# One-hot products of the gate stage as three bf16 products in place of one in float32

## The reference

```
s1, s2 = q[:, :, 0] @ k1.T, q[:, :, 1] @ k2.T          # 8 heads, 128 keys each
v1, i1 = top_k(s1, 16);  v2, i2 = top_k(s2, 16)
top_s, pos = top_k(v1[..., :, None] + v2[..., None, :], 16)
idx = i1 * 128 + i2   (of the chosen pairs)
g = softmax(top_s)                                     # 8 x 16 = 128 experts a token
y = sum over the 128 experts e:  g_e * gelu(x . u[idx_e]) * v[idx_e]
```

## Time and profile before

| | |
|---|---|
| time, median of 3 runs | 1710.99 us (1710.89 to 1716.2) |
| the profiled execution | 1710.73 us, span of its instructions 1708.9 us |
| TensorE busy, products / loads | 1635.4 us (96%) / 1420.3 us (83%) |
| VectorE, ScalarE, GpSimd busy | 1256.0 (73%), 644.1 (38%), 836.6 us (49%) |
| mean granted clock of TensorE | 0.988 |
| share of the last chain | PE 59% (L1620 30%, L845 22%, L833 5%, L1498 3%) |
| gate stage | about 540 to 1004 us; first loop from 600, second from 795 us |

### The profile page before, as it was taken

The page is one execution under the profiler, slowest core; times in us unless marked ns, Lnnn a source line. Parts: engine busy times, 40 slices in busy tenths (PEclk is TensorE's granted clock), DMA queues, the critical chain, the costliest instruction groups (busy, mean ns, idle before and its releaser), DMA issues.

```text
span 1708.9 us, 23340 instructions
## 1 busy us (share of the span) xinstructions
PE 1635.4 (96%) x8522; PEld 1420.3 (83%) x8522; DVE 1256.0 (73%) x2452; ACT 644.1 (38%) x1056; POOL 836.6 (49%) x542
## 2 busy tenths in 40 slices
PE   7999889699998999999999889999999999999996
PEld 5876644499998999999999888888888888888885
DVE  6667842368998988855886357778777778888876
ACT  3568740333424433432333233333333333333331
POOL 4734520194454378877877524445555563222201
PEclk9999999899999999999999999999999999999999
DMA  8436300433345578898789989998999989999972
GB/s 274 147 104 191 99 0 0 139 101 105 118 130 168 156 203 228 228 320 244 214 227 254 356 298 321 323 323 321 320 326 326 318 298 346 350 356 351 360 250 101
DMA packets 242897, 397.16 MB, mean 232 GB/s; under 512 B 33704, under 2 KB 173408, under 8 KB 242784
## 3 DMA queue, kind: packets, MB, share of 16 engines
q1 hardware_dynamic: 182816, 259.17, 44.6%
q0 software_dynamic: 55296, 134.31, 26.1%
q10 hardware_dynamic: 4672, 2.19, 0.5%
HBM read 349.40 MB, written 46.20 MB: 231 GB/s over the span
## 4 chain that ended last, share of the span: by engine, by line
PE 59%; DVE 4%; DMA 2%; POOL 1%; issue 1%; ACT 1%; SPq 0%; POOLq 0%; DVEq 0%; ACTq 0%
PE bank L1620 30%; PE bank L845 22%; PE bank L833 5%; PE bank L1498 3%; DMA u_raw<-in_peer_u 2%; POOL gate_matrix L213 1%; DVE sel_late L954 1%; DVE ut_lo L903 1%; POOL gathered L1005 0%; DVE hit_late L952 0%; DVE hit_late L945 0%; DMA gathered<-in_peer_u,expert_rows 0%; DVE gather_product L1017 0%; ACT L975 0%; DVE first L1422 0%
## 5 line engine op out<-in xcount | busy, mean ns | idle before, releaser
L845 PE MATMUL bank<-xhi,ut_hi 128*128 128x384 f32 x1024 | 354.4, 346 | 0.3 <-ACT gel L871 0.3
L845 PE MATMUL bank<-xhi,ut_lo 128*128 128x384 f32 x1024 | 344.2, 336 | 0.0
L845 PE MATMUL bank<-xlo,ut_hi 128*128 128x384 f32 x1024 | 344.0, 336 | 0.0
L1005 POOL DMA_INDIRECT gathered<-in_peer_v,expert_rows x128 | 199.8, 1561 | 259.5 <-DVE gather_sum L1021 240.6
L1005 POOL DMA_INDIRECT gathered<-in_peer_u,expert_rows x128 | 168.9, 1320 | 184.1 <-DVE gather_product L1017 158.1
L903 DVE TENSOR_TENSOR ut_lo<-bank,ut_hi 128x512 fp32r<-128x512 f32 x216 | 141.7, 686 | 154.2 <-ACT ut_hi L862 153.5
L213 POOL DMA_INDIRECT gate_matrix<-gate_values,gate_cells x128 | 224.1, 1751 | 56.7 <-issue 37.2
L1620 PE MATMUL bank<-v_hi,w_hi 128*128 128x512 f32 x768 | 240.5, 395 | 1.4 <-DVE w_lo L1717 1.4
L1620 PE MATMUL bank<-v_lo,w_hi 128*128 128x512 f32 x768 | 237.8, 391 | 0.0
L1620 PE MATMUL bank<-v_hi,w_lo 128*128 128x512 f32 x768 | 237.5, 391 | 0.0
L1654 ACT ACTIVATE v_hi<-gate_rows_then_feed 128x1024 fp32r<-128x1024 f32 x128 | 135.9, 1062 | 236.1 <-PE bank L1620 236.1
(11 more groups left out here) (197 smaller groups left out, 2506.1 us busy)
## 6 DMA issues: line engine op xcount, KB each, us to landing
u_raw<-in_peer_u SPq DMA_DIRECT2D x128, 512.0 KB, 5.2
gate_rows_then_feed<-in_peer_v SPq DMA_DIRECT2D x128, 512.0 KB, 7.4
gate_rows_then_feed<-gate_matrix SPq DMA_DIRECT2D x128, 192.0 KB, 4.9
activations<-gel SPq DMA_DIRECT2D x96, 192.0 KB, 3.1
gate_rows_then_feed<-activations SPq DMA_DIRECT2D x96, 192.0 KB, 6.1
w_in<-in_w_in SPq DMA_DIRECT2D x28, 512.0 KB, 4.2
gate_matrix<-gate_zeros SPq DMA_DIRECT2D x8, 1024.0 KB, 7.0
wq<-in_peer_wq SPq DMA_DIRECT2D x16, 512.0 KB, 4.4
```

The lines of the kernel that those rows point to most:

```text
L845: ins = self.nc.tensor.matmul(self.bank[b + (r % 2) * spare][:, 0:DTOK], u[r % 2][:, k, :], x[:, k, 0:DTOK], start=(i == 0), stop=(i == 3 ...
L1005: self.nc.gpsimd.indirect_dma_start(out=self.tile[r][:, :], out_offset=None, in_=self.tables[kind], in_offset=bass.IndirectOffsetOnAxis(ap ...
```

## The change

The one-hots are made in bf16 and with the four tokens of a group innermost (`[P, KEYS, NT]`). The gate, a float32, is split into three bf16 numbers that sum to it: ScalarE's copy to `selT` is now bf16 and gives the upper one, VectorE makes the two others in `pieces`, four instructions chained by waits, at the start of each loop. For a group VectorE now makes `first` without the gate, `second`, waits for `first`, and multiplies `first` by each of the three pieces; these are five instructions of 128 x 512 bf16. TensorE makes three bf16 products for each token, added up in PSUM, whose two operands are read with a step of four elements. A constant `each`, the key number four times over, is made once at the stage's start.

```diff
-        selT = sb("selT", [P, 3, P])
-        first = sb("first", [P, 2, NT, KEYS])
-        second = sb("second", [P, 2, NT, KEYS])
+        selT = sb("selT", [P, 2 + PIECES, P], BF16)
+        rest = sb("gate_rest", [P, 2, P])
+        each = sb("iota_each", [P, KEYS, NT], BF16)
+        second = sb("second", [P, 2, KEYS, NT], BF16)
+        piece = sb("first_pieces", [P, 2, PIECES, KEYS, NT], BF16)
...
             picks.constants(link)
+            link(V.tensor_copy(each[:, :, :], iota[:, :].unsqueeze(2).broadcast_to([P, KEYS, NT])))
...
+            def pieces(tb):
+                eng.wait_ge(selT_ready, tb + 1)
+                link(V.tensor_tensor(out=rest[:, 0, :], in0=bank[6][:, 2 * P:3 * P], in1=selT[:, 2, :], op=ALU.subtract))
+                V.sem_inc(pieces_ready, 1)
+                link(V.tensor_copy(selT[:, 3, :], rest[:, 0, :]))
+                link(V.tensor_tensor(out=rest[:, 1, :], in0=rest[:, 0, :], in1=selT[:, 3, :], op=ALU.subtract))
+                link(V.tensor_copy(selT[:, 4, :], rest[:, 1, :]))
+
             def one_hots(tb, i):
                 if i == 0:
-                    eng.wait_ge(selT_ready, tb + 1)
+                    pieces(tb)
                 for e in groups_of(i):
                     n, t, u = tb * GROUPS + e, e * NT, e % 2
                     after(eng, g_done, n - 1)
-                    shape = [P, NT, KEYS]
-                    V.tensor_tensor(out=second[:, u, :, :], in0=iota[:, :].unsqueeze(1).broadcast_to(shape),
-                                    in1=selT[:, 1, t:t + NT].unsqueeze(2).broadcast_to(shape), op=ALU.is_equal)
-                    for q in range(t, t + NT):
-                        ins = V.tensor_scalar(out=first[:, u, q - t, :], in0=iota[:, :], scalar1=selT[:, 0, q:q + 1],
-                                              scalar2=selT[:, 2, q:q + 1], op0=ALU.is_equal, op1=ALU.mult)
+                    of = lambda row: selT[:, row, t:t + NT].unsqueeze(1).broadcast_to([P, KEYS, NT])
+                    first = piece[:, u, PIECES - 1, :, :]
+                    V.tensor_tensor(out=first, in0=each[:, :, :], in1=of(0),
+                                    op=ALU.is_equal).then_inc(first_ready, 1)
+                    V.tensor_tensor(out=second[:, u, :, :], in0=each[:, :, :], in1=of(1), op=ALU.is_equal)
+                    eng.wait_ge(first_ready, n + 1)
+                    for p in range(PIECES):
+                        ins = V.tensor_tensor(out=piece[:, u, p, :, :], in0=first, in1=of(2 + p), op=ALU.mult)
                     ins.then_inc(hot_ready, 1)
...
-                    after(eng, selT_ready, tb)
+                    after(eng, pieces_ready, tb)
...
                         for q in range(NT):
-                            ins = nc.tensor.matmul(bank[4 + u][:, q * KEYS:(q + 1) * KEYS], second[:, u, q, :],
-                                                   first[:, u, q, :], start=True, stop=True)
+                            for p in range(PIECES):
+                                ins = nc.tensor.matmul(bank[4 + u][:, q * KEYS:(q + 1) * KEYS], second[:, u, :, q],
+                                                       piece[:, u, p, :, q], start=(p == 0), stop=(p == PIECES - 1))
                         ins.then_inc(g_done, 1)
```

More of the change, by code:

```diff
@@ L63 @@
 ST = DT - 1
-NT, PARTS = 4, 7
+NT, PARTS, PIECES = 4, 7, 3
 GROUPS = P // NT
@@ L1365, in gates @@
         hot_ready, g_done, g_copied = (sem(n) for n in ("one_hot_ready", "g_done", "g_copied"))
+        pieces_ready, first_ready = sem("gate_pieces_ready"), sem("first_one_hot_ready")
         g_stored = [sem("g_low_stored"), sem("g_high_stored")]
@@ L1462, in scalar @@
                     after(eng, hot_ready, tb * GROUPS)
-                    S.activation(selT[:, :, :], bank[6][:, 0:3 * P].rearrange("p (a t) -> p a t", a=3),
+                    S.activation(selT[:, 0:3, :], bank[6][:, 0:3 * P].rearrange("p (a t) -> p a t", a=3),
                                  ACT.Copy).then_inc(selT_ready, 1)
```

## The result

| | before | after |
|---|---|---|
| median of the runs made side by side | 1710.94 us (4 runs) | 1739.04 us (4 runs, 1736.79 to 1740.63) |
| ratio | | 1.0162, 95% interval 1.0141 to 1.0184 |
| profiled execution, span | 1710.73, 1708.9 us | 1736.79, 1735.0 us |
| TensorE / VectorE / GpSimd busy | 1635.4 / 1256.0 / 836.6 us | 1669.9 / 1263.0 / 828.2 us |

The change makes the kernel 28 us (1.6%) slower. Forecast was 1712, with a range that ended at 1724.

The account below looks back on a forecast made before the run. The prediction took GpSimd, slower than TensorE's step, to set the second gate loop's end, so TensorE's saving would not reach it: 1710.7 + 2 (held GpSimd starts) - 0.4 (shorter last bursts) = 1712.3, so 1712 us, range 1702 to 1724.

Parts of the forecast that it names:

- I take 56: Gate loops, TensorE: a bf16 product costs 56 ns, three 168 per token, 13.8 us less TensorE work.
- Rival B: Gate bursts: products cost 111 ns each through loads or strided reads, 28.4 us more TensorE work, 1738 us; chance 0.09.
- Rival C: Gate bursts: half of each weight load isn't hidden, 81 ns a product, 5.4 us more TensorE work, 1714.6 us; chance 0.10.
- 421 ns and 0.34 from start to start: Gate loops, VectorE: duration and spacing of each of the five one-hot instructions, 1.70 us a group.
- 1.4 us for the splitting: Start of each gate loop, VectorE: four chained instructions, about 0.35 us each; cost 0, at worst 1.4 us.
- Rival E: Gate loops, VectorE: one-hots run at one element a cycle, a step of 8.3 us, 1778 us; chance 0.04.
- GpSimd slower than TensorE: Gate loops: GpSimd needs 7.0 us a step against TensorE's 6.54, so TensorE's saving doesn't reach the end.
- the forecast 7: First gate loop: TensorE would gain 19 x 0.37 = 7 us, then stand waiting for the rest before the loop's end.
- the lead: End of the first gate loop: 2.2 us left of GpSimd's head start with gathered tiles, for TensorE to spend.
- The held starts, "+2": Gate loops: GpSimd issues held back by VectorE's two-input instructions, 2 us more, bounds 0 and 3.6.
- Rival D: Gate loops: GpSimd is kept out for a whole group of five VectorE instructions, 0.85 us a start, 1755 us; chance 0.05.
- Rival A: Gate loops: GpSimd's waits for landings shorten, up to 11 us gained, 1700 us; chance 0.22.

Follow-up runs that it names:

- flat_both: The changed kernel with both operands of the three products read as 128 neighbouring elements, tokens mixed up: 1712.0 us, ratio 1.0015 to the kernel before.
- flat_one: The changed kernel with contiguous operand reads and one product a token instead of three: 1719.28 us in a single run, beside 1717.43 for the kernel before.
- pairs: The changed kernel with two tokens innermost instead of four, so TensorE steps 4 bytes: 1713.95 us, ratio 1.0021 to the kernel before.
- before_latest: The kernel before with GpSimd issuing 1.8 scatters in a loop step instead of 2.2: 1702.09 us, ratio 0.9954.
- pairs_latest: The changed kernel with two tokens innermost and 1.8 scatters in a loop step instead of 2.2: 1696.38 us, ratio 0.9902 to the kernel before.
- step_eight: The changed kernel with weights contiguous and the moving operand read 16 bytes apart: 1863.32 us in a single run, beside 1717.43 for the kernel before.
- before_later: The kernel before with GpSimd issuing 2.0 scatters in a loop step instead of 2.2: 1702.7 us, ratio 0.9948.

## Why the prediction was wrong, point by point

**TensorE, the step that failed.** The term is the price of one bf16 product: "I take 56", between the bounds 56 and 111, and "reading every fourth element costs double" was only the upper one's reason. It measured 118 to 119, above even that bound. The choice rested on the weight load: that a one-pass load, 50 ns, fits under the product. flat_both bears that out at 56 ns, but it answers another question. A load that fits says nothing of how fast the strided operand is read, and no row of the trace of before has one. Rival B had the place, the mechanism (strided reads) and 1738 us; at 0.09 it was priced far too low, since its "against" was the same load argument. At 119 ns its own sum would be 256 x (357 - 222) = 34.6 less 1.5, so 1743.8; it is 1736.8 in the profiled execution, since TensorE's idle time in the second loop was nearer 2.8 and 5.6 us came back outside the loops.

The Trainium skill (SBUF — State Buffer, "Door 1: The DMA port swizzle", note on cachelines) says that up to 8 bf16 elements can be stepped for free, as long as a 16-byte line is hit twice. The runs disagree for TensorE's moving operand: 6 bytes cost 88 ns, 8 bytes 116 to 119, against 56 for contiguous reads. By it rival B would not have come about, and it did.

**Rival C and its page.** The pace with a load each, in bursts of 24, is 56 to 58 ns, not 81. The figure of the Trainium skill (TensorE: Matmul & The Clock Gate, "Back-to-back issue gap"), about 81 ns for a load and a product of 128 columns in a stream, was not met here; its formula for a single one gives 55.8, which was.

**VectorE.** 421 ns and 0.34 from start to start, and 1.4 us for the splitting, all held. The timeline of after, from the first of the four splitting instructions on:

```profile
598.86 0.29 DVE L1417 TENSOR_TENSOR gate_rest<-bank,selT 128x128 f32<-128x128 f32 x1 [2.44 <-ACT selT L1477]
...
600.22 0.43 DVE L1432 TENSOR_TENSOR first_pieces<-iota_each,selT 128x512 bf16<-128x512 bf16 x1
600.57 0.42 DVE L1434 TENSOR_TENSOR second<-iota_each,selT 128x512 bf16<-128x512 bf16 x1
600.90 0.42 DVE L1437 TENSOR_TENSOR first_pieces<-first_pieces,selT 128x512 bf16<-128x512 bf16 x1
```

598.86 to 600.22 is 1.36 us, then three one-hot instructions 0.35 and 0.33 apart. Rival E falls with this. No cost of the splitting shows in the profiled execution of after, whose first product starts 1.2 us earlier than before. But over all traces that start lies at 603.2 to 606.7 us with the splitting and at 603.5 to 604.4 without, so a cost of about 1 us isn't ruled out.

**GpSimd slower than TensorE.** Right, but only seen once the products were made cheap. In flat_both the second loop starts 4.8 us earlier than before and ends at 918.6 against 920.8, "within 3 us of where it does now"; in flat_one, with 28.7 us more taken away, it ends no earlier but at 927.6. The first loop gained 4.9 us (pairs 5.7) of the forecast 7, about what it gains with GpSimd out of the way (5.4 from before_latest to pairs_latest). VectorE did wait for gathered tiles there, as forecast, 5.8 us in three places, but only 1.1 us of it reached TensorE. So that part was misread: what was left of the lead, 2.2 us, did not bound TensorE's gain in that loop. In the second TensorE idled 8.2 us against 1.5, where about 10 more were expected.

**The held starts, "+2".** Not borne out. The 52 issues of the first loop took the same 98 us, and in the two stretches of the earlier trace rows flat_both has 117 issues in 177.97 us of busy time, 1.52 each; before had 116 in 179.02, 1.54 each. The term is between 0 and -3, though which issues are in the stretch differs a little. Rival D, which would add 0.85 us to each, falls: in the second stretch flat_both has 98.03 / 66 = 1.49.

**The sum.** With this layout it is 1739. With the products at the price that it assumed, it was 1712.3 and flat_both measured 1712.0 in the median, ratio 1.0015. That agreement is partly luck: the "+2" in the sum was not borne out, flat_both's ten runs spread over 16 us, and its profiled execution, at 1706.81, is the fastest of them.

**Rival A** (the gain comes through) falls in flat_both and flat_one. It needed a change to GpSimd's queue, and then came through by half (5.7 of 256 x (222 - 3 x 58) ns = 12.3 us).

## What to carry to other kernels

A layout that is contiguous for the engine that writes is strided for the one that reads: before a product's operand is laid out, ask for the step in bytes of the moving one. Here 4 bytes were free and every byte more cost in proportion, while the weights' step cost next to nothing, so two bf16 numbers innermost served both engines. And where an engine off the chain is nearly as slow as the one on it, a faster operation is worth nothing until that one's load is cut too; cut it first and alone, since that brought 8 us here by itself (before_latest, 0.9954) and the products 6 more.

## What was not expected of the hardware

- The moving operand's cost in proportion to its step from 4 bytes on (58, 88, 116 to 119, 227 ns for 4, 6, 8, 16 bytes), and for 16 bytes the same at a mean granted clock of 0.81 and of 1.00.
- The two operands differ: the same 8-byte step adds 60 ns a product on the moving operand and 1 to 3 on the weights.
- In step_eight the granted clock stood at 0.84 to 0.88 in the loops while TensorE was busy without a gap, and unstrided work behind the bursts of 24 paid for it (1.71 us instead of 0.88 for 8 transposes). What in the strided products brings it down was not tried apart.
- GpSimd's queue weighed on the kernel before more than its waits showed: 0.2 scatters a step fewer in the loops brought some 9 us, where its waits in the second loop left TensorE idle for 1.5. In the trace of before_later 5 us of it lie behind the second loop, in that of before_latest 2; why there was not settled.
